# Both gating products of a two-block model by Strassen's scheme: seven block products in place of eight

## The reference, cut to what matters

```
h = h + (p[i] @ ple_w_up[i]) * jax.nn.sigmoid(h @ ple_w_gate[i])
```

## Time and profile before

| | us |
|---|---|
| median of 3 runs | 2906.77 |
| lowest and highest | 2902.79, 2908.14 |
| the profiled execution's own time | 2910.77 |
| its span | 2909.0 |
| TensorE busy in the span | 2794.4 (96%) |
| VectorE, ScalarE, GpSimd busy | 1189.2, 904.1, 1022.1 |

### The profile page before, as it was taken

The page is one execution under the profiler, slowest core; times in us unless marked ns, Lnnn a source line. Parts: engine busy times, 40 slices in busy tenths (PEclk is TensorE's granted clock), DMA queues, the critical chain, the costliest instruction groups (busy, mean ns, idle before and its releaser), DMA issues.

```text
span 2909.0 us, 41142 instructions
## 1 busy us (share of the span) xinstructions
PE 2794.4 (96%) x16908; PEld 2166.7 (74%) x16908; DVE 1189.2 (41%) x2813; ACT 904.1 (31%) x1701; POOL 1022.1 (35%) x447
## 2 busy tenths in 40 slices
PE   7979999899999999998999999999999999999998
PEld 5756676667777777776887878888888888887887
DVE  6998996556433333335335011111112121114423
ACT  5412233552334343335123222222222222224112
POOL 2532383133322222223542433333333333333631
PEclk8979899999999999999999999999999999999999
DMA  4100021031211111112211111111111111113211
GB/s 110 42 22 22 22 73 62 36 97 43 66 26 48 52 51 52 51 44 88 65 66 61 55 44 37 45 44 44 37 51 45 37 45 44 44 44 139 66 51 65
DMA packets 221334, 155.56 MB, mean 53 GB/s; under 512 B 25254, under 2 KB 207948, under 8 KB 221020
## 3 DMA queue, kind: packets, MB, share of 16 engines
q1 hardware_dynamic: 210076, 122.55, 14.6%
q10 hardware_dynamic: 11072, 30.39, 3.0%
HBM read 133.45 MB, written 19.47 MB: 53 GB/s over the span
## 4 chain that ended last, share of the span: by engine, by line
PE 51%; DVE 1%; issue 1%; ACT 1%; DMA 0%; ACTq 0%; DVEq 0%
PE proj L903 14%; PE proj L905 14%; PE proj L904 14%; PE out L1420 2%; PE score L1368 1%; PE score L1398 1%; PE score L1377 1%; PE proj L943 1%; PE out L904 0%; PE out L905 0%; PE out L903 0%; PE out L1387 0%; DMA y_scratch<-arena 0%; DVE arena L2332 0%; DVE arena L2459 0%
## 5 line engine op out<-in xcount | busy, mean ns | idle before, releaser
L903 PE MATMUL proj<-act_hi,w_hi 128*128 128x512 f32 x2560 | 1032.7, 403 | 13.2 <-ACT hT L1835 7.2
L905 PE MATMUL proj<-act_hi,w_lo 128*128 128x512 f32 x2560 | 1005.5, 393 | 0.0
L904 PE MATMUL proj<-act_lo,w_hi 128*128 128x512 f32 x2560 | 1005.0, 393 | 0.0
L776 POOL TENSOR_TENSOR w_hi<-w_raw,ones 128x1024 fp32r<-128x1024 f32 x175 | 419.7, 2398 | 1603.9 <-PE proj L905 1601.5
L903 PEld LDWEIGHTS proj<-act_hi,w_hi 128*128 128x128 f32 x2560 | 486.4, 190 | 127.2 <-issue 21.3
L905 PEld LDWEIGHTS proj<-act_hi,w_lo 128*128 128x128 f32 x2560 | 485.2, 190 | 104.8
L904 PEld LDWEIGHTS proj<-act_lo,w_hi 128*128 128x128 f32 x2560 | 486.0, 190 | 95.9 <-issue 0.2
L778 POOL TENSOR_TENSOR w_lo<-w_raw,w_hi 128x1024 fp32r<-128x1024 f32 x175 | 433.8, 2479 | 13.7
L1835 ACT ACTIVATE arena<-proj 128x512 f32<-128x512 f32 x236 | 176.0, 754 | 659.7 <-PE proj L905 635.7
L2459 DVE SCALAR_TENSOR_TENSOR arena<-arena,score 128x256 f32<-128x256 f32 (+1 forms) x192 | 76.1, 427 | 718.5 <-PE score L1368 676.8
L1861 ACT ACTIVATE arena<-score 128x512 f32<-128x512 f32 (+3 forms) x264 | 115.8, 487 | 195.5 <-PE score L1229 195.1
(11 more groups left out here) (268 smaller groups left out, 2881.5 us busy)
## 6 DMA issues: line engine op xcount, KB each, us to landing
w_raw<-dil_w_in_dram SPq DMA_DIRECT2D x80, 512.0 KB, 3.7
w_raw<-fox_w_in_dram SPq DMA_DIRECT2D x32, 512.0 KB, 4.2
w_raw<-w_in_dram SPq DMA_DIRECT2D x23, 512.0 KB, 3.9
y_scratch<-arena ACTq DMA_DIRECT2D x21, 512.0 KB, 3.6
act_lo<-y_scratch SPq DMA_DIRECT2D x21, 512.0 KB, 5.9
arena<-decay_scratch ACTq DMA_DIRECT2D x16, 512.0 KB, 5.7
w_raw<-ple_w_gate_dram SPq DMA_DIRECT2D x16, 512.0 KB, 3.7
arena<-x_dram SPq DMA_DIRECT2D x12, 512.0 KB, 5.3
```

The source lines that it names most:

```text
L776: pool.tensor_tensor(hi, raw, one.unsqueeze(1).broadcast_to([P, KB, P]), ALU.mult).then_inc(w_hi_done, 1)
L903: pe.matmul(bank, hi, a_hi, start=first, stop=False)
L904: pe.matmul(bank, hi, a_lo, start=False, stop=False)
L905: return pe.matmul(bank, lo, a_hi, start=False, stop=last)
```

## The change

Half of a gate's matrices are taken as blocks: A11, A12, A21, A22 of the residual (first digit the half of tokens, second the half of the features 0 to 3 and 4 to 7), and the weights of tile pair r, which are the tiles r and r+4. For each of the 4 pairs, 7 products of 4 rows (12 matmuls) replace 4 x 24 matmuls. The moving sides are A11, A12, A22 and four sums: S1 = A21+A22, S2 = S1-A11, S4 = A12-S2, S3 = A11-A21. The stationary sides are three raw blocks and four differences, made by DVE in place in w_raw (`weight_turn`, four per pair), each then split by POOL in halves of the old size (512 columns) through a ring of four (`gate_splits`). Sums of products are formed by letting a product accumulate onto an ACT copy of an earlier one from bank to bank (`onto`), and by DVE adding an ACT copy (`aside`, `joined`).

- *TensorE.* New order in `ple`: pair 0 is P1, up 11, P5, P6, up 22, P3, P2, P7, then P1 of pair 1, up 12, P4 of pair 0, up 21; pairs 1 to 3 are P1, P5, P2, up 11, P6, up 12, P3, P7, up 22, P4, up 21. The up product has the same 96 matmuls per gate.
- *DVE.* The sums S1, S2, S4 of row k are made in the output pass of tile k+4, each followed by its lo part. The last tile's part is made after the pass:

```diff
             def residual_parts(m):
...
+                for j in range(KB - 1):
+                    residual(m, j, 0)
+                    if j < 4:
+                        residual_lo(m, "A11", j)
+                    residual(m, j, 1)
+                    if j >= 4:
+                        for half in range(2):
+                            dve.wait_ge(pass_free[half], C_OUT[m] + j + 1)
+                        combined_parts(m, j - 4)
+                weight_turn(m, 0, 3)
+                weight_turn(m, 0, 1)
+                weight_turn(m, 0, 2)
+                residual(m, KB - 1, 0)
+                p_lo(m, 0)
+                for k in range(2):
+                    combine(m, "S3", k, hT[:, k, 0:512], hT[:, k, 512:T], ALU.subtract)
+                for k in range(2):
+                    residual_lo(m, "A12", k)
+                    residual_lo(m, "A22", k)
+                    part_lo(m, "S3", k, whole_part("S3", k))
+                residual(m, KB - 1, 1)
+                for half in range(2):
+                    dve.wait_ge(pass_free[half], C_OUT[m] + KB)
+                combined_parts(m, 3)
+                p_lo(m, 1)
+                for k in range(2, 4):
+                    residual_lo(m, "A12", k)
+                for k in range(2, 4):
+                    combine(m, "S3", k, hT[:, k, 0:512], hT[:, k, 512:T], ALU.subtract)
+                    part_lo(m, "S3", k, whole_part("S3", k))
+                weight_turn(m, 0, 4)
+                for k in range(2, 4):
+                    residual_lo(m, "A22", k)
...
+            def gate_pair(m, r, first=(), second=(), third=()):
+
+                add_gated_squares(first)
+                gated(m, r, "11")
+                add_gated_squares(second)
+                joined(m, r, "12")
+                gated(m, r, "12")
+                joined(m, r, "22")
+                add_gated_squares(third)
+                if r + 1 < GATE_PAIRS:
+                    weight_turn(m, r + 1, 3)
+                    weight_turn(m, r + 1, 1)
+                gated(m, r, "22")
+                if r + 1 < GATE_PAIRS:
+                    weight_turn(m, r + 1, 2)
+                if r < GATE_PAIRS - 1 or m == 2:
+                    gated(m, r, "21")
+                if r + 1 < GATE_PAIRS:
+                    weight_turn(m, r + 1, 4)
```

```diff
+                if ks[0] == 0:
+                    later(pe, PL[m], "wlo", n + 1)
...
+                    if name in ("P3", "P7"):
+                        later(pe, PL[m], "onto", 2 * r + 2)
...
+                    if name == "P4":
+                        later(pe, PL[m], "sum", sum_at(r, "22") + 1)
...
+                for k in ks:
+                    if r == 0:
+                        later(pe, PL[m], "lo", GATE_PARTS.index((GATE_MOVING[name], k)) + 1)
```

More of the change, by code:

```diff
@@ L186, in gated @@
         out.extend([None, None])
-        plain(4 + 8)
+        plain(4)
     plain(2)
@@ L715, in up_and_gate @@
                     out_block(m, j)
-                for j in range(8):
-                    whole(W_GATE[m] + j, col(w_gate[m - 1], j * P), (W_GATE[m] + j) % 2)
+                for r in range(GATE_PAIRS):
+                    gate_weights(m, r)
             for j in range(2):
@@ L912, in weight_ready, with half_T @@
                     pe.wait_ge(w_split, n + 1)
-            def half_T(n, c, slot, half, part=None, bank=None, parts=None, inside=None):
+            def half_T(n, c, slot, half, part=None, bank=None, inside=None):
                 ks = range(KB) if part is None else range(part * KB // 2, (part + 1) * KB // 2)
@@ new lines, in squares @@
+            def squares(which):
+                for j, half in which:
+                    tok = slice(half * 512, half * 512 + 512)
+                    mates, _ = square_adds(j, half)
+                    n = len(mates)
+                    later(act, PL[1], "h", quarter_at(j % 4, f"{half + 1}{j // 4 + 1}") + 1)
+                    if (j, half) == GATE_SQUARES[0]:
+                        later(act, PL[1], "used", product_at(GATE_PAIRS - 1, "P1") + 1)
+                    if n >= 3:
+                        later(act, ND, "acc", adds_to(mates[n - 2]))
+                    act.activation((dsq[n % 2] if n else dacc)[:, tok], hT[:, j, tok], ACT.Square).then_inc(ND["sq"], 1)
@@ L2720, in _ @@
             residual_parts(2)
-            for j in range(KB):
-                for half in range(2):
-                    gated(2, j, half)
+            for r in range(GATE_PAIRS):
+                gate_pair(2, r)
             dve.wait_ge(FIN["gain"], 16)
```

526 lines of the change are left out of this document (384 added, 142 removed).

## The result

| | us |
|---|---|
| after, median of 4 runs | 2926.11 (2922.72 to 2932.62) |
| before, median of 4 runs beside them | 2907.45 (2902.79 to 2908.79) |
| ratio, 95% interval | 1.007 (1.0049 to 1.0091) |
| profiled execution of after: time, span | 2932.6, 2930.8 |

A forecast was written before the change was run, and what follows sets the result against it. TensorE's matmuls were taken as the bound, busy in 96% of the span. 96 fewer matmuls (-22.4), gate waits (+30.0) and the end of gate 1 (+10.0) gave +17.6 us: median 2924, range 2897 to 2937.

The forecast's parts named there:

- rival B: Waits smaller: gate 1's end costs 5, and 864 stage matmuls keep the output passes' 0.227 pace, -5.2 us; 2914, chance 0.18.
- P5 waits for S1's row 3: Start of each gate: TensorE waits 8.7 us in P5's fourth row for a lo part queued late on VectorE.
- clock after it: Each gate: the granted clock falls after the 8.7 us wait, costing 1.6 us in slow matmuls.
- P1 of pair 1: Each gate: the second pair's weights are split late, so TensorE waits 1.4 us (0 to 1.4).
- P4 of pair 0: Each gate: P4's bank must first be read by quarter 22's join, queued behind quarter 12 on VectorE; 2.5 us.
- pair 1's splits: Each gate: TensorE catches up with a chain of weight differences and splits of P5 and P2; 0.8 us.
- end of gate 1: Pair 3 through first_two: late quarter 11, token sums, spread and smaller delays cost +10 us, about +5 if nothing meets.
- rest of the end: End of gate 1: P3's copy 0.8 late, first_two's wait 0.8 longer, second half's spread delaying VectorE 1.5 us.
- rival A: GpSimd's splits hardly hinder VectorE: start wait 2.0 us, each gate loses 4.8, the end 5; 2899, chance 0.17.
- Rival C: Pairs in step wait too: 1 us at P3 and at P4 in 6 pairs, +12; 2936, chance 0.11.
- P1 starts unhindered: Start of a gate: p's lo part is done at -0.2 us, so P1's first matmul has no wait.
- no reader for 8 heads: 0: Stores of x_scratch cost nothing, since nothing reads them for 8 heads; 0 us.

The follow-up runs named there:

- hold_splits: The changed kernel, but GpSimd's second row of splits in each gate waits until S1's row 3 is done; median 2931.7 us, ratio to before 1.0082.
- squares_in_psum: The changed kernel, but ScalarE writes most of gate 1's squares into two free PSUM banks; median 2925.7 us, ratio to before 1.0067.
- all_edits: The changed kernel with reordered gate starts, five roundings on ScalarE, an earlier quarter 22 join, squares in PSUM and a reordered gate 1 end; 2896.5 us, ratio 0.9965.
- gate_reads_act_rows: The kernel before, but gate 2's tiles 1 to 7 multiply act_hi rows in place of the residual's parts; median 2906.0 us, ratio 0.9995.
- squares_and_order: squares_in_psum plus another order at gate 1's end: root before the last squares, second half's token sums and spread earlier; 2922.1 us, ratio 1.0049.
- quarter_11_first: end_rearranged with quarter 11 gated after two A22 lo parts, stores spread out, one more rounding on ScalarE, row 2's rounding earlier; 2891.4 us, ratio 0.9942.
- split_alone: all_edits, but VectorE waits before A22's lo parts until GpSimd has split the weights of P1 of pair 1; 2898.0 us, ratio 0.9966.
- end_rearranged: split_alone with gate 1's end reordered again, GpSimd's first split for the next mixer held until quarter 22 is added; 2896.9 us, ratio 0.9961.

## Why the prediction was right, and where it was off

**The sum, term by term.** The differences of the stretches between the profiled executions are +16.8 (gate 1 and its end), +2.6 (gate 2), and 2.5 elsewhere (+0.8 before gate 1, +1.0 in the dilated mixer, +0.7 behind gate 2), which no step of the prediction covers and which is small beside the 10 us by which executions differ in their early stages. Forecast were +13.8, +3.8 and 0. A wait below is the gap between two starts less 0.23.

| term | forecast | measured |
|---|---|---|
| 96 matmuls less | -22.4 | -22.4: 96 counted, at the old pace |
| pace of the 864 that stay | 0 (rival B: -5.2) | -5.5 |
| per gate: P1's start | 0 | 0.7 |
| P5 waits for S1's row 3 | 8.7 | 8.4 |
| clock after it | 1.6 | 2.0 |
| P1 of pair 1 | 1.4 | 1.3 |
| P4 of pair 0 | 2.5 | 2.4 |
| pair 1's splits | 0.8 | 0.8 in gate 1; none in gate 2, but the clock fell after P4's wait, 1.6 |
| end of gate 1: quarter 11 | 1.6 | 2.1 |
| token sums | 1.6 | 1.5 |
| spread | 3.8 | 3.5 |
| rest of the end | 3.1 | 7.1 |

A gate's waits sum up to 16.5 us beyond the pace (in gate 2, 427 starts in 113.3 us; the same number of steps at 0.2267 makes 96.8), where 15.0 were forecast.

**The step that decided was right.** VectorE's last add of tile 7 was forecast at +11.4 after the first gate matmul and started at +11.0; S1's lo part was forecast to be done at +15.0 and P5's fourth row started at +14.6. Its price, 1.67 us for a meeting from one pair of rows of 1024 columns, held at 512 columns (1.68 to 1.75). One count was off by one: six operations met a split, not seven. hold_splits showed the cause by taking the meetings away. With it **rival A falls** (its wait was 2.0). The Trainium skill's page "SBUF — State Buffer", section "SBUF: two separate sides", has the lock taken by a VectorE operation with two SBUF inputs and by whichever engine starts first. The rows agree, and squares_in_psum agrees from the other side. Who goes next when both have work queued is open: at the start of a gate the two alternate, while three instructions of GpSimd's were kept out for over 3 us by rows of VectorE's.

**Rival C falls**: from the end of pair 0's last waits (1503) to pair 3 no wait is over 0.1 us. **Rival B** was half right: the pace came down as it said, and the end of gate 1 cost more, not 5.

**Wrong: "P1 starts unhindered."** The walk put p's lo part at -0.2, so P1 was free by a hair; it ended 0.1 us before P1's first matmul, which came 0.65 late. A margin of 0.2 us at the end of a walk of eleven operations is no margin. P1 writes into the PSUM bank from which p's lo part is made, and waits for it. all_edits moved p's part up by one place and the wait went.

**Unsure, and it stayed so: the clock after a short wait.** The prediction put it at nothing behind 2 us, with 1.6 as a bound. Both came: P4's wait of 2.4 us is followed by a clock of 1.00 in gate 1 (1494.0 to 1500.0) and by 0.67 in gate 2 (2835.8 to 2841.0), 1.6 us. Which of the two follows is not told by the length of the wait.

**Mis-sized: the end of gate 1**, +10 forecast. The gate 1 stretch less what gate 2 shows, 16.8 - 2.6, says +14.2. Of the waits that were walked through three came out near the forecast; the fourth, P3's for its copy, 0.8, left no gap in the trace. Not in the sum were: the clock, which falls again after the waits for quarter 11 and for the spread (priced only at P5, though the same row was at hand), 3.4 us more of slow matmuls than in the profile of before; the issue of four stores on ScalarE's queue, for which I wrote "no reader for 8 heads: 0" and looked at the data only, not at the 2.9 us that stand before row 2's rounding; and VectorE idle for 2.1 us behind ScalarE's root and 2.6 behind the second spread, against 1.6 in all before, so 3.0 more, where 1.5 were taken. The 14.2 is itself uncertain by the clock: against the gate 1 stretch of gate_reads_act_rows, 146.9 with the same instructions as before, it is 11.6. squares_in_psum (-4.8), squares_and_order (-2.3 more) and quarter_11_first show that most of it was order and place, not the number of squares: in the last, with all 16 squares still in pair 3, the same difference (-7.8 in gate 1 less -9.6 in gate 2) is 1.8.

**Wrong: gate stages keep their pace.** The prediction left the 0.006 us per matmul to rival B because no row said why the pace changes. That hid 5.5 us of gain. The sum came close by luck in this part: the end of gate 1 cost 4.2 us more than forecast and each gate's waits 1.5 more, and the pace gave back 5.5.

## What to carry to other kernels

When work on tensors in SBUF is given to VectorE, count its two-input operations beside GpSimd's instructions in the same stretch: each pair that met here cost VectorE 1.0 us and GpSimd 0.3 to 0.5, so halve one side (ScalarE can round) or put one operand in PSUM. A mathematical saving on TensorE is real only if what feeds its first consumers is in time: here the waits of the two gates, 2 x 16.5 us, ate the 28 us that fewer matmuls and the pace gave, and taking them away by order and by engine gave 2891 in place of 2926. When a wait is taken away, look at what stands behind the moved operation on its queue; it is where the time turned up again three times.

## What was not expected of the hardware

- VectorE's operations with two SBUF inputs, in a row without a gap, kept an instruction of GpSimd's out for the rest of the row three times: 5.19, 4.55 and 4.59 us for an instruction of 1.28, and 2.21 once the row was cut short. It is no rule: at the start of a gate, and at 1463.91 in all_edits, GpSimd was let in after a single operation of such a row. What decides is open.
- An add with one input in PSUM ran through GpSimd's splits at 0.67 to 0.69 us, as if they weren't there.
- The same matmul, 128 by 512 on the same weights, has a pace of 0.233 or 0.227 us depending on the moving rows, with the granted clock at 1.00 in both.
- ScalarE copies 512 columns from PSUM to PSUM in 0.58 to 0.60 us, and to SBUF in 0.57 to 0.60: the bound of twice the time that the prediction set beside its forecast of nothing wasn't needed.
- The same waits of TensorE's aren't always followed by the same clock. At the head of `first_two`, with the instructions of the kernel before, 3.5 us at 0.56 or 9.8 at 0.50; behind the waits of 2.26 and 1.11 us in gate 1, 13 matmuls with about 0.43 us between starts follow in split_alone, and none in end_rearranged.
